# Value and output projection of the causal mixers, cut into blocks between the heads' steps

## The reference, cut to what matters

```python
h = h + 0.5 * swiglu(rmsnorm(h, ffn1_norm), ...)        # feed-forward 1
hn = rmsnorm(h, mix_norm)
qkv = hn @ w_qkv                                        # 1024 -> 3 x 1024, first mixer
# second mixer: q = hn @ b_w_q; k, v = rmsnorm(h_stream) @ kv_w
p = softmax(q @ k.T * 64 ** -0.5 + mask)                # causal, each of 16 heads
h = h + (p @ v).reshape(256, 1024) @ w_o                # output projection
h = h + 0.5 * swiglu(rmsnorm(h, ffn2_norm), ...)        # feed-forward 2
```

## Time and profile before

| | |
|---|---|
| median of 3 runs | 2063.09 us (2062.91 to 2064.02) |
| the profiled execution's own time | 2064.49 us |
| its span, first to last instruction | 2062.8 us |
| TensorE busy in the span | 1984.9 us (96%) |
| VectorE, ScalarE, GpSimd busy | 1096.2, 939.7, 170.6 us |
| mean granted TensorE clock | 0.978 of full speed |

### The profile page before, as it was taken

How to read it: one execution, slowest core, us unless ns; L and a number is a source line. 1 busy time by engine, 2 the same in 40 slices (tenths; PEclk the granted TensorE clock), 3 DMA queues, 4 the chain that set the end, 5 groups by cost and what they waited for, 6 DMA issues and landing times.

```text
span 2062.8 us, 26200 instructions
## 1 busy us (share of the span) xinstructions
PE 1984.9 (96%) x9100; PEld 1591.8 (77%) x9100; DVE 1096.2 (53%) x1326; ACT 939.7 (46%) x1248; POOL 170.6 (8%) x269
## 2 busy tenths in 40 slices
PE   5999999998999999999999999999999999999998
PEld 4777878886877878887788886788878887667886
DVE  4565665546566565445544446544464555435544
ACT  3564454435455454444444446444454444444442
POOL 5210000001311000000100031000020001000000
PEclk9999999999999999999999999999999999869999
DMA  5334465554413546554555552455555555205552
GB/s 180 115 108 145 171 200 183 183 183 137 162 62 123 196 166 212 185 183 160 182 189 191 171 171 105 142 195 188 183 175 172 184 194 182 102 23 182 183 184 101
DMA packets 202779, 332.72 MB, mean 161 GB/s; under 512 B 11328, under 2 KB 150208, under 8 KB 202688
## 3 DMA queue, kind: packets, MB, share of 16 engines
q1 hardware_dynamic: 198320, 319.86, 46.0%
q0 software_dynamic: 3264, 11.54, 1.7%
q10 hardware_dynamic: 1104, 0.16, 0.1%
HBM read 330.47 MB, written 1.05 MB: 161 GB/s over the span
## 4 chain that ended last, share of the span: by engine, by line
PE 61%; issue 31%; DVE 4%; POOL 2%; ACT 2%; DMA 1%; POOLq 0%; ACTq 0%; DVEq 0%
PE ps L492 17%; PE ps L496 17%; PE ps L494 17%; PE ps L667 3%; PE ps L646 3%; PE ps L504 2%; PE ps L655 2%; DVE wlo L1435 1%; DVE h L1473 1%; ACT whi L1013 1%; POOL stat L1912 1%; POOL stat L1913 1%; DMA freq<-freq_dram 1%; ACT prob L1044 0%; DVE xs L1812 0%
## 5 line engine op out<-in xcount | busy, mean ns | idle before, releaser
L1435 DVE TENSOR_TENSOR wlo<-raw,whi 128x2048 fp32r<-128x2048 f32 (+1 forms) x304 | 686.6, 2259 | 593.8 <-ACT whi L1013 593.7
L1013 ACT ACTIVATE whi<-raw 128x2048 fp32r<-128x2048 f32 (+2 forms) x308 | 581.1, 1887 | 463.4 <-PE ps L496 458.5
L492 PE MATMUL ps<-whi,act_hi 128*128 128x512 f32 (+1 forms) x1632 | 620.2, 399 | 23.5 <-DVE act_lo L1441 23.4
L494 PE MATMUL ps<-wlo,act_hi 128*128 128x512 f32 (+1 forms) x1632 | 606.8, 391 | 0.0
L496 PE MATMUL ps<-whi,act_lo 128*128 128x512 f32 (+1 forms) x1632 | 606.8, 391 | 0.0
L492 PEld LDWEIGHTS ps<-whi,act_hi 128*128 128x128 f32 x1632 | 306.9, 190 | 91.7 <-DVE act_lo L1441 27.8
L496 PEld LDWEIGHTS ps<-whi,act_lo 128*128 128x128 f32 x1632 | 309.4, 190 | 65.7
L494 PEld LDWEIGHTS ps<-wlo,act_hi 128*128 128x128 f32 x1632 | 309.9, 190 | 60.8
L1054 ACT ACTIVATE hid<-ps 128x256 f32<-128x256 f32 x132 | 50.7, 384 | 274.4 <-PE ps L504 200.6
L492 PE MATMUL ps<-whi,hid_hi 128*128 128x512 f32 x544 | 168.3, 390 | 1.8 <-DVE h L1473 1.8
L496 PE MATMUL ps<-whi,hid_lo 128*128 128x512 f32 x544 | 167.6, 389 | 0.0
(11 more groups left out here) (194 smaller groups left out, 1717.3 us busy)
## 6 DMA issues: line engine op xcount, KB each, us to landing
raw<-ffn_w_gate_dram SPq DMA_DIRECT2D x88, 512.0 KB, 4.0
raw<-ffn_w_up_dram SPq DMA_DIRECT2D x88, 512.0 KB, 5.0
raw<-ffn_w_down_dram SPq DMA_DIRECT2D x88, 512.0 KB, 3.9
raw<-w_in_dram SPq DMA_DIRECT2D x64, 512.0 KB, 4.3
raw<-w_ffn_gate_dram SPq DMA_DIRECT2D x44, 512.0 KB, 4.0
raw<-w_ffn_up_dram SPq DMA_DIRECT2D x44, 512.0 KB, 5.1
raw<-w_ffn_down_dram SPq DMA_DIRECT2D x44, 512.0 KB, 3.8
raw<-a_w_qkv_dram SPq DMA_DIRECT2D x24, 512.0 KB, 4.4
```

Source lines behind the costliest of these rows:

```text
L492: nc.tensor.matmul(o, hi, a, start=start, stop=False)
L494: nc.tensor.matmul(o, hi, a, start=False, stop=False)
L1013: nc.scalar.activation(whi[:, u % SLOTS, 0:words], raw[:, u % SLOTS, 0:words], ACT.Copy)\
L1435: nc.vector.tensor_tensor(wlo[:, u % SLOTS, 0:words], raw[:, u % SLOTS, 0:words], whi[:, u % SLOTS, 0:words].bitcast(F32), ALU.subtract)\
```

## The change

In both causal mixers the value projection is divided into two halves of 512 columns (c = 0 and 1). Its four units no longer hold two K tiles of all columns, but four K tiles of one half. `value_block(c, j, t)` is 12 matmuls: half c, K tiles 4j to 4j+3, token tile t. The four blocks of c = 0 come first, with the transposes of keys or queries after the first product and inside the third block, and the first two scores in the fourth. The four blocks of c = 1 are put behind steps 0 to 3 of the heads. The output projection becomes eight blocks by K tile (`output_block(p)`, 12 matmuls: K tile p, which is pair p of the heads, both token tiles). Blocks 0 to 5 are put behind steps 5, 7, 9, 11, 13 and 15, blocks 6 and 7 behind the last step. The turned probabilities use bank 2 alone, the pairs bank 3 alone.

ScalarE's and VectorE's splits of the next weight units, which before stood ahead of the heads (VectorE: 9, then one behind the keys and one in step 0) and behind them (3 on each), are distributed over the heads' steps: on ScalarE behind head 0 and in steps 2, 5, 8 and 12, on VectorE in steps 1, 3, 5, 8 and 12. The sum of the splits is the same. ScalarE copies the values in four parts of 512 columns instead of two of 1024.

```diff
+++ after.py
...
@@ -648,11 +656,15 @@
...
-                    free_before("turn", tn)
+                    if causal:
+                        was_read("turn", tn - 1)
+                    else:
+                        free_before("turn", tn)
+                    bank = 2 if causal else 2 + tn % 2
...
+                def causal_output():
+                    pair, odd = sc // 2, sc % 2
+                    if not odd and pair % (H2 // 2):
+                        was_read("pair", pair - 1)
+                    was_read("turn", tn)
+                    o = ps[VD * odd:VD * (odd + 1), 3, 0:S]
+                    for kt in range(T):
...
@@ -939,16 +964,73 @@
...
+            def value_block(c, j, t, hi, lo, steps=None):
+
+
+                unit, half = u + 2 * c + j, hf + 2 * c + t
+                if t == 0:
+                    unit_there(unit)
+                if j == 0:
+                    free_before("half", half)
+                vh, vl = u_view(whi, unit, 4, D // 2), u_view(wlo, unit, 4, D // 2)
+                for k in range(4):
+                    kt = 4 * j + k
+                    if steps and (j, t, k) in steps:
+                        steps[j, t, k]()
+                    last = product([ps[:, 4 + 2 * t, :]], hi[:, kt, t * P:(t + 1) * P], lo[:, kt, t * P:(t + 1) * P],
+                                   [vh[:, k, :]], [vl[:, k, :]], kt == 0, kt == DT - 1)
+                if j == 1:
+                    last.then_inc(sem("half_done"), 1)
+                elif t == T - 1:
+                    last.then_inc(sem("used"), 1)
+
+            def output_block(p, pair, tiles=range(T)):
+
+
+                unit, k = u + p // 2, p % 2
+                if 0 in tiles:
+                    was_read("pair", pair + p)
+                    if k == 0:
+                        unit_there(unit)
+                vh, vl = u_view(whi, unit, 2, D), u_view(wlo, unit, 2, D)
+                for t in tiles:
+                    if p == 0:
+                        free_before("half", hf + t)
+                    last = product([ps[:, 4 + 2 * t + n, :] for n in range(2)],
+                                   o2_hi[:, p, t * P:(t + 1) * P], o2_lo[:, p, t * P:(t + 1) * P],
+                                   [vh[:, k, n * 512:(n + 1) * 512] for n in range(2)],
+                                   [vl[:, k, n * 512:(n + 1) * 512] for n in range(2)], p == 0, p == DT - 1)
+                    if p == DT - 1:
+                        last.then_inc(sem("half_done"), 1)
+                    elif (k, t) == (1, T - 1):
+                        last.then_inc(sem("used"), 1)
...
+            def mix(heads, pair, hi, lo, steps):
...
+                nonlocal u, hf
+                for j in range(2):
+                    for t in range(T):
+                        value_block(0, j, t, hi, lo, steps)
...
+                others = {2 * j + t: lambda j=j, t=t: value_late(j, t) for j in range(2) for t in range(T)}
+                others.update({2 * p + 5: lambda p=p: output_block(p, pair) for p in range(H2 // 2 - 2)})
+                attend(heads, values, others)
+                heads[-2][2]()
+                heads[-1][1]()
+                output_block(H2 // 2 - 2, pair, (0,))
+                heads[-1][2]()
+                output_block(H2 // 2 - 2, pair, (1,))
+                output_block(H2 // 2 - 1, pair)
+                u, hf = uo + 4, ho + T
...
-            steps = {(0, 4 + e): lambda e=e: turn_k(e) for e in range(4)}
-            steps.update({(1, 5): first_score, (1, 6): heads[1][0]})
-            wide_here(act_hi, act_lo, beside(steps))
-            attend(heads, 2, hf - 1)
...
+                steps = {(0, 0, 1 + e): lambda e=e: turner(e) for e in range(2)}
+                steps.update({(1, 0, 2 + e): lambda e=e: turner(2 + e) for e in range(2)})
+                steps.update({(1, 1, 1): first_score, (1, 1, 3): heads[1][0]})
...
+            mix(heads, 0, act_hi, act_lo, beside_values(turn_k))
...
@@ -1335,7 +1417,7 @@
...
+            def attend(sc):
+
+
+                nonlocal tn, hf
+                copy_values(0, 0)
+                exps(sc, causal=True)
+                copy_values(0, 1)
+                split(1)
+                for s in range(1, H2 + 2):
                     if s < H2:
                         exps(sc + s, causal=True)
                     if s >= 2 and s % 2:
@@ -1371,7 +1464,12 @@
                         pair_hi((sc // 2) + pair, o2_hi[:, pair, :])
                     if 1 <= s <= H2:
                         probs_turned(sc + s - 1, tn + s - 1, True)
+                    if s in (3, 4):
+                        copy_values(1, s - 3)
+                    if s in (2, 5, 8, 12):
+                        split(1)
...
@@ -1562,7 +1654,8 @@
 
             def pair_lo(pair, dst, hi):
                 dve.wait_ge(sem("pair_hi"), w.at("pair_hi", pair + 1))
-                rest(dst, ps[:, 5 + 2 * (pair % 2), 0:S], hi).then_inc(sem("pair_read_v"), 1)
+                src = ps[:, 3 if w.layer is None else 5 + 2 * (pair % 2), 0:S]
+                rest(dst, src, hi).then_inc(sem("pair_read_v"), 1)
...
-            def turn_keys():
+            def turn_keys(between=0):
                 nonlocal tn
                 for t in range(T):
                     for g in range(2):
                         turned_copy(tn + 2 * t + g, kT2[:, 4 * g:4 * g + 4, t * P:(t + 1) * P])
+                    if t == 0:
+                        split(between)
...
@@ -1849,23 +1944,21 @@
 
                         pair = (s - 3) // 2
                         pair_lo(sc // 2 + pair, o2_lo[:, pair, :], o2_hi[:, pair, :])
-                    if s == 0:
-                        split(early)
                     if 1 <= s <= H2:
                         normalise(sc + s - 1, ("expd", sc + s), causal=True)
+                    if s in (1, 3, 5, 8, 12):
+                        split(1)
...
-            split(9)
-            hf += 3 * T
+            split(8)
+            hf += 4 * T
             tn += 4
-            turn_keys()
-            split(1)
-            attend(0, 1, early=1)
-            split(3)
+            turn_keys(between=1)
+            attend(0, 1)
```

More of the change, by code:

```diff
@@ L164, in unit_ends, with values @@
     per_layer, used = used, 0
[L165 to L169, removed]
+    def values(hf):
+        return [*wide(2, hf), *wide(2, hf + 2)]
+    two = ffn(0, 0) + wide(4, 2) + wide(4, 4) + values(6) + wide(4, 10)
+    two += ffn(2 * NCH, 12) + wide(4, 14) + ffn(4 * NCH, 16)
+    two += wide(4, 18) + values(20) + wide(4, 24) + ffn(6 * NCH, 26)
     return one, two, per_layer
@@ L438, in _ @@
             u += UNITS_FFN
-            for n in range(3):
+            for n in range(2):
                 for j in range(4):
@@ L442, in _ @@
                 u += 4
+            for i in range(4):
+                v = u_view(raw, u + i, 4, D // 2)
+                load(u + i, [(v[:, k:k + 2, :], block("a_w_qkv_2", 0, 4 * (i % 2) + k, 2,
+                                                     2 * D + i // 2 * (D // 2), D // 2)) for k in (0, 2)])
+            u += 4
             for j in range(4):
@@ L670, in output, with attend @@
                         last.then_inc(sem("pair_done"), 1)
[L672 to L674 removed]
+                def causal_output():
[5 more added lines that the diff above has]
+                    for kt in range(T):
+                        last = nc.tensor.matmul(o[:, kt * P:S], v[:, kt], probT[:, sc % 2, kt, kt * P:S],
+                                                start=kt == 0, stop=kt == T - 1)
+                    if odd:
+                        last.then_inc(sem("pair_done"), 1)
+                return score, turn_probs, causal_output if causal else output
+            def attend(heads, values, others):
                 n = len(heads)
                 for s in range(n):
[L680 to L682 removed]
+                    if 1 <= s < n - 1:
+                        heads[s + 1][0]()
                     if s == 2:
[L684 removed]
+                        was_read("half", values + T - 1)
+                    if s == 2 + n // 2:
+                        was_read("half", values + 2 * T - 1)
                     if s >= 2:
@@ L980, in _ @@
             heads = heads_here(H2)
[L981 to L985, removed]
+            mix(heads, H2 // 2, o2_hi, o2_lo, beside_values(turn_q))
             ffn_here()
@@ L1347, in copy_out @@
                 for t in range(T):
-                    if t == 1 and between is not None:
-                        between()
                     half_there(hf + t)
```

90 lines of the change are left out of this document (46 added, 44 removed).

## The result

The changed kernel takes 2081.09 us (median of 4 runs, 2079.82 to 2082.06) against 2063.0 us for the kernel before (4 runs beside it, 2062.19 to 2064.02). The ratio is 1.0087, 95% interval 1.007 to 1.0105: slower, by 18.1 us. The prediction was 2083, 19.5 us above the kernel before. The profiled execution took 2082.06 us, with a span of 2080.4 (before: 2062.8).

The account below looks back on a forecast made before the run. TensorE, busy 96% of the span, was taken to bound the kernel. First mixer +24.2 and second -4.7 gave +19.5 on the median 2063.09: 2082.6, rounded 2083 us; range 2066 to 2096, likeliest case 2074 to 2092.

Parts of the forecast that it names:

- The splits inside the heads: In each mixer's heads TensorE waits behind VectorE's splits of steps 5, 8 and 12: 11.1 us of pause.
- The first rival: In the heads, VectorE's splits do not hold TensorE up, so their pauses and clock cost go: 2048 us; chance 0.11.
- The seam: Before feed-forward 2, token tile 0's normalising chain loses cover: 3.6 us of pause per mixer, plus 1.7 of clock.
- The front: At the first mixer's start, TensorE waits for key rotation (1.9) and turned keys (1.3): 3.2 us, plus 0.8 of clock.
- The pauses taken away: In the mixers, blocks cover all TensorE's old pauses: 2.26 us saved in the first, 2.82 in the second.
- step (a): Value block 2 covers the mixers' first wait, the blocks behind it the end waits; 2.26 and 2.82 us go.
- The lower clock of the second mixer: In the second mixer, 24.4 us go if the clock stays up.
- the clock term of the prediction: In the heads, pauses of 4.5 us cost 2.0 each (a block follows at once), that of 2.1 costs 2.1.
- The clock behind the new pauses: Longer pauses bring TensorE's clock down: 8.6 us in the first mixer, 7.8 in the second, seam's 1.7 included.
- The third rival: Each new pause in both mixers brings the clock down at the highest cost: +33.0 us, 2096; chance 0.12.
- The weight loads and the switches of format: Weight queue and block seams in both mixers: taken as 0; switches bounded by 0 and 2 us in both mixers.

Follow-up runs that it names:

- experiment 1: Changed kernel with VectorE's splits in the heads at steps 1, 3, 7, 9 and 13 instead of 1, 3, 5, 8 and 12; 2046.96 us.
- experiment 3: Changed kernel with first key (second mixer: query) transposes one value block later and VectorE's split behind all turned-key copies; 2077.74 us.
- experiment 2: Changed kernel with output blocks 4 and 5 doing only token tile 0 in their steps and the end reordered to close that tile early; 2077.69 us.
- experiment 7: Changed kernel with VectorE's splits at steps 1, 3, 7, 9 and 16, token tile 0 first at the end, and later key transposes; 2036.81 us.
- experiment 5: Kernel before, without blocks, with VectorE's split of step 0 moved behind the first normalising in both mixers; 2037.13 us.
- experiment 8: Kernel before, without blocks, with turned probabilities in bank 2 alone and pairs in bank 3 alone; 2063.7 us.
- experiment 4: Changed kernel with VectorE's splits at steps 1, 3, 7, 9 and 13, token tile 0 first at the end, and later key transposes; 2042.3 us.

## Why the prediction was right

It named the sign, the size and the places. Point by point, against the profiled executions:

**The splits inside the heads** carried the forecast: 11.1 us a mixer, as 4.5 + 4.5 + 2.1. Measured: 4.44 + 4.44 + 2.05 = 10.93, in both mixers. The chain was added up from durations of before, and the shape of the argument (VectorE works its list in order, so what stands behind a waiting split waits too) is what experiment 1 shows by moving the splits alone. The first rival, that the splits don't hold the heads up, gave 2048; the kernel of experiment 1, in which they indeed don't, takes 2046.96.

**The seam**: 3.6 predicted, 3.61 measured, twice. **The front**: 1.9 + 1.3 = 3.2 predicted, 1.75 + 1.46 = 3.21 measured, in the first mixer alone as said.

**The pauses taken away**: 2.26 and 2.82 were too much. The pause of 0.64 at an output near the end stayed in each mixer, for ScalarE's copy of the turned probabilities (step (a) had the blocks cover it). The timeline of the changed kernel in its first mixer:

```profile
1324.22 0.55 PE L667 MATMUL ps<-ident,prob 128*128 128x128 f32 x3
1325.41 0.86 PE L690 MATMUL ps<-probT,v 128*64 128x256 f32 x4 [0.64 <-ACT probT L1194]
1326.21 0.55 PE L667 MATMUL ps<-ident,prob 128*128 128x128 f32 x3
1326.51 0.71 PE L500 MATMUL ps<-whi,o_hi 128*128 128x512 f32 x2
```

The scores are all done there, the step before it has its block and the step behind it too, but between these transposes and their output stands nothing. That is 1.3 us more than forecast in both mixers.

**The lower clock of the second mixer** went as predicted, though a pause of 2.05 and two of 4.44 stand in its heads. Its mean clock is 0.95 now. Behind each of these pauses a block of 512-column matmuls follows within a few steps, as the clock term of the prediction had it, and the clock is full again; that the blocks are the cause was not tried apart.

**The clock behind the new pauses**, 6.9 us in the first mixer and 6.1 in the second without the seam's part: TensorE's busy time rose by 6.2 in the first (86.87 - 80.63); in the second, where 24.4 of the 105.07 were the old lower clock, it is 85.50 - (105.07 - 24.4) = 4.8. The seam, 1.7 predicted: 1.2 and 1.3. The front, 0.8 predicted, is inside the 6.2; no stretch at the lower clock follows the two waits of 1.75 and 1.46, so it is 0. All the clock's terms together: 16.4 predicted, 6.2 + 4.8 + 1.2 + 1.3 = 13.5 measured, the largest error of the sum. Part by part the first mixer comes to +23.5 with its seam (predicted +24.2), the second to -5.9 (-4.7): +17.6 (+19.5). The errors are +1.3 (pauses that stayed), -2.9 (clock) and -0.3 (the three pauses a mixer): -1.9.

The Trainium skill ("TensorE: Matmul & The Clock Gate", section "A second HAM failure mode: psum-queue depth-cycling") tells of TensorE's clock swinging when it often idles briefly between groups. In the changed kernel every pause of the mixers from 2.05 us up has a stretch at the lower clock behind it, and those of 1.75, 1.46 and 0.64 have none. By that rule the trace agrees in part again. Experiment 3 goes against it once: the pause of 2.05 us of its first mixer has no such stretch. The third rival, which took every pause at its dear end, gave 2096 and was 15 us too high.

That the clock's terms came so near is in part luck. The same six pauses in the heads (2.05, 4.44 and 4.44 in each mixer) had some 24 us at the lower clock behind them in the changed kernel, 37 in experiment 2 and 31 in experiment 3. At most half of that is lost, 12, 19 or 15 us, against 12.2 in the forecast (4.0 + 2.1, twice).

**The weight loads and the switches of format**, taken at nothing: experiment 7 has all the blocks and experiment 5 has none, and both run their mixers at a clock of 1.00. In the second mixer TensorE is busy 80.78 us in experiment 7 and 80.74 in experiment 5, in 82.29 and 82.27 us. No cost of either shows above 0.1 us.

What the forecast left unsaid is what the change is worth when done well. The blocks save no matmul. With its splits, keys and seam mended the changed kernel reaches 2036.81; the kernel before with one split moved reaches 2037.13, and their ranges meet. Neither run improves on the other by more than the measurement tells. What both removed is the long pauses.

## What to carry to other kernels

On an engine that works its list in order, background work has its price in what stands behind it, not in its own length: put it where its input is ready and the others have work for as long as it takes. To price such a placement, add the chain's durations from the trace and take off the other engine's work in that stretch; here that met three pauses to within 0.1 us.

When the clock of TensorE is low through a long stretch of small matmuls, look for the pause ahead of it before restructuring: here one instruction moved gave 26 us, as much as the whole rearrangement at its best.

Try combined edits as a set: what one uses as cover another may take away.

## What was not expected of the hardware

A pause of 1.99 us cost 24.4 us, as the clock stayed at 0.50 through the heads behind it. It did so again in experiment 8 (58 us at the lower level in the second mixer). In the changed kernel pauses of 4.44 us in the same stage cost some 1.7 each, with blocks of wide matmuls behind them. All other stretches at the lower level, in all kernels read here and the end of the span apart, came in lengths near 3.4, 6.8 or 10.2 us (by windows of half a microsecond), but which of them follows a given pause changed. The pauses of 4.44 us in the second mixer were followed by 3.4 in the changed kernel and by 6.8 in experiment 2; that of 2.05 in the first mixer by 6.8 in the changed kernel and by none in experiment 3; and a pause of 1.31 us by 6.8 in one mixer of experiment 4 and by none in the other. No run here tells why. It is the part of such a forecast that has to stay a range.
